# A merged front stage and attention scores computed two steps ahead, in a two-block transformer kernel on one core

## The chip, the cores and the metric

The kernel runs on one core of a Trainium2 chip: TensorE (PE), VectorE (DVE), ScalarE (ACT), GpSimd (POOL), the queue engine SyncE (SP) and 16 DMA engines. The metric is the time of one execution in microseconds, from the device; the median of three runs counts.

## The reference, cut to what matters

Two transformer blocks over 512 tokens of width 1024, in fp32. Only the first half of the first block is touched:

```python
mod = silu(c) @ w_ada + b_ada                     # 1024 x 6144
shift1, scale1, gate1, shift2, scale2, gate2 = split(mod, 6)
h = rms_norm(x, norm1_g) * (1 + scale1) + shift1
q_g, k_g, v_g, a_lr, r_g, q_s, k_s, v_s = split(h @ w_in)
log_a = log_sigmoid(a_lr @ w_gla_alpha + b) / 16
o_gla = rms_norm(gla_mixer(q_g, k_g, v_g, log_a)) * silu(r_g)   # gated linear attention, 4 heads
o_swa = rms_norm(swa_mixer(q_s, k_s, v_s, sinks))               # sliding window, 8 heads, 2 key heads
x = x + gate1 * (concat(o_gla, o_swa) @ w_out)
```

After that come the product-key expert layer (`peer_mixer`: a gather of expert rows), and the second block with its two attentions and its feed-forward. None of them is changed.

## The kernel before

Activations lie feature-first: `K.xres[:, k, :]` holds features 128k to 128k + 127 of all 512 tokens. Products with weights are made in three TensorE passes (`split_product`, L115 to L117): ScalarE rounds a weight tile to its high part (`high`, L269), GpSimd makes the low part (`lows`, L274), and high x high, high x low and low x high are added. `Columns` keeps three raw, three high and three low tiles; load n waits for low n - 3, high n for the product of tile n - 3.

The program is a row of stages, each a block in which every engine runs its own list, with a barrier between blocks. Those concerned:

1. `stage_setup` (0 to 51 us). SP loads x and the first 2048 columns of w_ada (shift1 and scale1) in eight tiles; ScalarE queues 23 small loads, among them c, which TensorE turns with all other vectors before ScalarE's Silu. TensorE turns x into `K.xres`. VectorE makes bias rows and masks, then adds up c times w_ada in 16 operations of 128x1024 (L480, L483), TensorE sums these over the partitions in 16 columns (L110), VectorE gets modT and g1.
2. `stage_in1` (51.6 to 229 us). The norm of x (`Norm`: squares on ScalarE L139, sums on TensorE L110, root L150 and L153, scale on VectorE L158), shift and rounding (L569), low part (L623). Then 16 column tiles (0 to 3 q and k of the linear attention, 4 the gate's rank, 5 to 12 r and the window's q, 13 and 14 its keys, 15 its values) and four row tiles for v_g. VectorE evicts tiles 4, 13, 14 and 15, ScalarE the others; tile n waits for the eviction of tile n - 2. Beside it VectorE adds up the other 4096 columns of w_ada in 32 operations (L632, L635) from a ring of two buffers, all of them ahead of its copy of the keys (L649) in its list; TensorE turns these sums after row tile c = 2.
3. `stage_mixers` (229 to 406 us). Two attentions are woven: `weave` sorts each engine's pieces by a place number that each generator yields. `Gla` has seven levels of 11 units: offsets of the log decay on VectorE (L753), two passes on ScalarE (L711, L713), factors qe and ke on VectorE (L789, L790), 16 products on TensorE (L110), taken under a mask into the scores (L762). After them an eighth product, decayed keys, states and outputs. `Swa` has 16 steps of 7.5 units, one block of 128 queries for two heads each: scores on TensorE; first() on VectorE: bias, row maximum, sink (L968 to L972); exps on ScalarE (L1007); second() on VectorE: sum, reciprocal and scaling of the probabilities (L976 to L979); turn on TensorE (L925), copy on ScalarE (L1015), product with the values on TensorE. The scores of step i + 1 are asked for at the start of step i and wait for the bias adds of step i; their two heads use partitions 0 to 63 and 64 to 127.

Then `stage_out1`, `stage_peer_scores` and the rest follow, unchanged.

## Time and profile before

| | us |
|---|---|
| median of 3 runs | 2811.97 |
| lowest, highest | 2810.17, 2816.26 |
| the profiled execution | 2816.42 |
| its span, first to last instruction | 2814.5 |
| `stage_setup` | 0 to 51.2 |
| `stage_in1` | 51.6 to 229.0 |
| `stage_mixers` | 229.0 to 406.2 |

All rows below are of the profiled execution. PE and the like with a q behind it are the engine's queue. A group's row gives line, engine, operation, out<-in, shapes, count, then busy time and mean ns of one, then how long the engine stood idle before these instructions and who ended that. A timeline row merges instructions alike: start, how long from the first's start to the last's end, count, and in brackets the idle time before it. Matmul records: an fp32 product is two records; on TensorE records overlap, so a mean can be longer than the distance from one to the next.

### The profile page before, as it was taken

To read this page: it belongs to the slowest core of one execution; us is meant where nothing else is said; L and a number is where in the kernel's file an instruction comes from. 1 tells how busy PE (TensorE), PEld (TensorE's weight loads), DVE (VectorE), ACT (ScalarE), POOL (GpSimd) and SP (SyncE) were. 2 spreads that over 40 slices of the span, in tenths; PEclk is the share of its full clock that TensorE was granted. 3 is DMA by queue.
4 is the path that set the end of the run, shared out by engine and by line. 5 is a ranking of instruction groups with operands and counts; after the bars stand their busy time and mean duration, and the time that the engine had idled before them with its cause. 6 is when DMAs were issued, how large, how long until landed. Compare 5 with 4: busy or idle time off the path is not lost. (4 is left out here: it accounts for less than half of the span.)

```text
span 2814.5 us, 22283 instructions
## 1 busy us (share of the span) xinstructions
PE 2132.3 (76%) x7265; PEld 1304.5 (46%) x7265; DVE 1515.5 (54%) x3605; ACT 674.4 (24%) x1202; POOL 1166.4 (41%) x774
## 2 busy tenths in 40 slices
PE   3875668861777777777788897767877997778899
PEld 2664446750322322222344443323336885646687
DVE  5535642119888678876788976555651112253111
ACT  2212343100000000000212112233214444444443
POOL 2320011311444444444466663322426885502687
PEclk7985578985999999999899998878998998879999
DMA  5640012334999999999999998977984664401465
GB/s 203 198 146 0 1 40 73 100 108 183 417 421 419 417 403 421 420 403 422 364 418 390 420 415 325 383 305 279 402 341 150 186 188 152 124 1 41 146 181 156
DMA packets 145864, 714.97 MB, mean 254 GB/s; under 512 B 13791, under 2 KB 39386, under 8 KB 79194
## 3 DMA queue, kind: packets, MB, share of 16 engines
q0 software_dynamic: 73728, 536.90, 46.8%
q1 hardware_dynamic: 69200, 172.38, 19.2%
q10 hardware_dynamic: 2826, 4.34, 0.4%
q8 instruction: 54, 0.88, 0.1%
q14 instruction: 56, 0.46, 0.1%
HBM read 701.77 MB, written 11.80 MB: 254 GB/s over the span
## 5 line engine op out<-in xcount | busy, mean ns | idle before, releaser
L1581 PE MATMUL ps<-uv_ring_a,expert_diag_a 128*128 128x512 f32 x2048 | 987.7, 633 | 392.9 <-DVE expert_diag_a L1472 392.8
L1364 POOL DMA_INDIRECT uv_ring_a<-in_peer_uv_dram,expert_idx x512 | 579.6, 1132 | 845.9 <-PE ps L1581 757.4
L1581 PEld LDWEIGHTS ps<-uv_ring_a,expert_diag_a 128*128 128x128 f32 x2048 | 396.3, 201 | 961.6 <-DVE expert_diag_a L1472 515.4
L1521 DVE CUSTOM_DVE_ANT_0 uv_ring_a<-uv_ring_a,x_rows 128x1024 f32<-128x1024 f32 x512 | 648.8, 1274 | 210.9 <-DMA uv_ring_a<-in_peer_uv_dram,expert_idx 208.8
L1652 POOL TENSOR_TENSOR w_low_b<-w_raw_b,w_high_b 128x1024 fp32r<-128x1024 f32 x98 | 234.7, 2397 | 236.3 <-ACT w_high_b L1646 234.9
L1564 ACT ACTIVATE expert_gelu_a<-expert_dot_a 128x2 f32<-128x2 f32 x256 | 52.1, 203 | 1054.4 <-DVE expert_dot_a L1521 1054.1
L1652 POOL TENSOR_TENSOR w_low_r<-w_raw_r,w_high_r 128x1024 fp32r<-128x1024 f32 x74 | 177.2, 2395 | 75.3 <-ACT w_high_r L1646 74.0
L1472 DVE TENSOR_SCALAR expert_diag_a<-ident,expert_weight_a 128x128 f32<-128x128 f32 x512 | 131.9, 314 | 15.0 <-PE ps L1581 5.6
L1646 ACT CAST w_high_b<-w_raw_b 128x1024 fp32r<-128x1024 f32 x98 | 102.8, 1051 | 119.0 <-PE ps L1665 119.0
L274 POOL TENSOR_TENSOR out_low<-out_raw,out_high 128x1024 fp32r<-128x1024 f32 x8 | 19.1, 2401 | 229.6 <-ACT out_high L269 229.6
L1646 ACT CAST w_high_r<-w_raw_r 128x1024 fp32r<-128x1024 f32 x74 | 77.9, 1055 | 85.2 <-PE ps L1665 85.0
L274 POOL TENSOR_TENSOR in_low<-in_raw,in_high 128x1024 fp32r<-128x1024 f32 x20 | 49.8, 2492 | 97.5 <-ACT in_high L269 97.5
L2387 DVE SCALAR_TENSOR_TENSOR ffn_silu_b<-ffn_silu_b,ps 128x256 f32<-128x256 f32 x22 | 9.2, 417 | 145.4 <-ACT ffn_silu_b L2369 145.4
L1663 PE MATMUL ps<-w_high_r,turned_high_r 128*128 128x512 f32 x208 | 82.2, 395 | 6.2 <-POOL w_low_r L1652 4.4
L1663 PE MATMUL ps<-w_high_b,turned_high_b 128*128 128x512 f32 x208 | 83.9, 403 | 3.8 <-DVE turned_low_b L1701 3.8
L2387 DVE SCALAR_TENSOR_TENSOR ffn_silu_r<-ffn_silu_r,ps 128x256 f32<-128x256 f32 x22 | 9.2, 418 | 140.7 <-ACT ffn_silu_r L2369 140.7
L220 POOL TENSOR_TENSOR peerq_low<-peerq_raw,peerq_high 128x1024 fp32r<-128x1024 f32 x16 | 38.0, 2378 | 110.8 <-ACT peerq_high L209 110.8
L1665 PE MATMUL ps<-w_high_b,turned_low_b 128*128 128x512 f32 x208 | 83.4, 401 | 0.0
L1664 PE MATMUL ps<-w_low_b,turned_high_b 128*128 128x512 f32 x208 | 83.4, 401 | 0.0
L1665 PE MATMUL ps<-w_high_r,turned_low_r 128*128 128x512 f32 x208 | 81.8, 393 | 0.0
L1664 PE MATMUL ps<-w_low_r,turned_high_r 128*128 128x512 f32 x208 | 81.7, 393 | 0.0
L115 PE MATMUL ps<-h_high,in_high 128*128 128x512 f32 (+1 forms) x128 | 52.1, 407 | 33.5 <-DVE kTd L649 17.2
(457 smaller groups left out, 3502.3 us busy)
## 6 DMA issues: line engine op xcount, KB each, us to landing
w_raw_r<-in_w_gu_dram SPq DMA_DIRECT2D x44, 512.0 KB, 3.8
w_raw_b<-in_w_gu_dram SPq DMA_DIRECT2D x44, 512.0 KB, 3.6
wada_rest<-in_w_ada_dram SPq DMA_DIRECT2D x32, 512.0 KB, 4.4
w_raw_a<-in_w_in_dram SPq DMA_DIRECT2D x24, 512.0 KB, 8.0
w_raw_b<-in_w_in_dram SPq DMA_DIRECT2D x24, 512.0 KB, 3.9
w_raw_r<-in_w_down_dram SPq DMA_DIRECT2D x22, 512.0 KB, 3.7
w_raw_b<-in_w_down_dram SPq DMA_DIRECT2D x22, 512.0 KB, 3.6
in_raw<-in_w_in_dram SPq DMA_DIRECT2D x20, 512.0 KB, 5.6
```

The source lines that it names most:

```text
L115: nc.tensor.matmul(out, w[0], x[0], start=first, stop=False)
L274: pool.tensor_tensor(self.lo[n % self.SPLIT][:, :], self.raw[n % self.RAW][:, :], self.hi[n % self.SPLIT][:, :].bitcast(F32), ALU.subtract ...
L1364: pool.indirect_dma_start(out=self.ring[:, n % self.RING, :], out_offset=None, in_=K.uv, in_offset=bass.IndirectOffsetOnAxis(ap=K.idx[self ...
L1472: dve.tensor_scalar(self.diag[q % self.DIAGS][:, :], K.ident[:, :], self.w[:, n % SLOTS:n % SLOTS + 1], None, ALU.mult).then_inc(self.s_di ...
L1521: dve.tensor_tensor_reduce(u, u, self.h[b][:, :], 1.0, 0.0, ALU.mult, ALU.add, self.a[:, s:s + 1]).then_inc(self.s_dot, 1)
L1564: act.activation(self.gl[:, c], self.a[:, c], ACT.Gelu).then_inc(self.s_gelu, 1)
L1581: ins = nc.tensor.matmul(self.bank(half), self.diag[q % self.DIAGS][:, :], self.ring[:, n % self.RING, D + 512 * half:D + 512 * half + 512 ...
L1646: act.copy(self.hi[n % self.SPLIT][:, :, :], self.raw[n % self.RAW][:, :, :]).then_inc(self.s_hi, 1)
L1652: pool.tensor_tensor(self.lo[n % self.SPLIT][:, :, :], self.raw[n % self.RAW][:, :, :], self.hi[n % self.SPLIT][:, :, :].bitcast(F32), ALU ...
L1663: nc.tensor.matmul(bank, rh, hi[:, kk, :], start=first and kk == 0, stop=False)
L1664: nc.tensor.matmul(bank, rh, lo[:, kk, :], start=False, stop=False)
L1665: ins = nc.tensor.matmul(bank, rl, hi[:, kk, :], start=False, stop=last and kk == self.KK - 1)
```

## The change

`stage_setup` and `stage_in1` become one block, `stage_front`:

- c is handed in as columns and loaded straight into its tile, as ScalarE's first load; the Silu follows on ScalarE before half of the small loads.
- w_ada's first part comes in 16 blocks of 128x1024, the scale half first, through a ring of six buffers lying in tiles that are written later; the other 32 blocks through a ring of three, then five.
- squares, sums and root of x follow the turning of x at once; GpSimd multiplies x by the inverse root (eight operations), and when g1 is there ScalarE scales and shifts in one operation and rounds in a second.
- the bias rows, masks and other constants are made between the sums; VectorE makes 28 of the 32 sums before the copy of the keys and four after the copy of the values; TensorE turns the sums after row tile c = 1.

In the mixers:

- the offsets and the zeroing of the level scores move from VectorE to GpSimd; TensorE's products of a level are four pieces half a unit apart.
- a step's two heads are now of the same half (0 to 63 or 64 to 127), their scores lie in one bank, the bank changes with the step, and the scores of step i + 2 are asked for in step i; one bias add serves both heads; the scaling of the probabilities moves from VectorE to ScalarE, before the turn.
- rows of w_out and of the window's norm gain are reordered on the host to fit.

```diff
+        ring1 = [rq_flat[:, D * r:D * r + D] for r in range(4)] + [qk_flat[:, D * r:D * r + D] for r in range(2)]
+        ring2 = own + [sums1[:, D * r:D * r + D] for r in range(2)]
+        MOD1 = [(k, c) for c in (1, 0) for k in range(KD)]
+        MOD2 = [(k, c) for k in range(KD) for c in range(4)]
...
+            for m, (k, c) in enumerate(MOD1):
+                if m >= len(ring1):
+                    sp.wait_ge(s_a1, m - len(ring1) + 1)
+                sp.dma_start(ring1[m % len(ring1)], I["w_ada"][0, k * P:(k + 1) * P, c * D:(c + 1) * D]) \
+                    .then_inc(s_w1[m % len(ring1)], 16)
+            for n in range(w.RAW):
+                w.load(sp, n)
...
+            turn = w.RAW
+            for m, (k, c) in enumerate(MOD2):
+                if m == len(own):
+                    sp.wait_ge(s_m1, 2)
+                if m >= len(ring2):
+                    sp.wait_ge(s_a2, m - len(ring2) + 1)
+                sp.dma_start(ring2[m % len(ring2)], I["w_ada"][0, k * P:(k + 1) * P, (2 + c) * D:(3 + c) * D]) \
+                    .then_inc(s_w2[m % len(ring2)], 16)
+                if m % 2:
+                    w.load(sp, turn)
+                    turn += 1
+            sp.dma_start(K.grow[:, :], I["b_ada"][0, 5 * D:6 * D].partition_broadcast(P)).then_inc(s_bg, 16)
+            for n in range(turn, len(w.src)):
+                w.load(sp, n)
...
+            pool.wait_ge(nm.s_inv, 1)
+            for k in range(KD):
+                pool.tensor_tensor(K.hT[:, k, :], K.xres[:, k, :], rs[:, :], ALU.mult).then_inc(s_xn, 1)
+            w.lows(pool, 0, 6)
+            pool.wait_ge(s_xn, KD)
+            step(pool.iota(dist, [[-1, 256]], base=P, channel_multiplier=1, allow_small_or_imprecise_dtypes=True))
...
+            w.lows(pool, 6, len(w.src))
...
+            act.dma_start(K.cact[:, :], I["c_columns"]).then_inc(s_c, 16)
...
+            act.wait_ge(s_c, 16)
+            act.activation(K.cact[:, :], K.cact[:, :], ACT.Silu).then_inc(s_silu, 1)
+            act.preload_act_table_set("natural_log_exp_and_others")
...
+            nm.squares(act, [(s_xe, k // 2 + 1) if k % 2 == 0 else (s_xd, k // 2 + 1) for k in range(KD)])
+            nm.root(act)
...
+                act.wait_ge(s_xn, k + 1)
+                act.activation(K.hT[:, k, :], K.hT[:, k, :], ACT.Identity, scale=K.g1[:, k:k + 1],
+                               bias=shift[k]).then_inc(s_h, 1)
+                act.wait_ge(s_h, k + 1)
+                act.copy(hi[:, k, :], K.hT[:, k, :]).then_inc(s_hh, 1)
...
+            for c in range(2):
+                pe.wait_ge(s_a1, KD * (c + 1))
+                for n in range(KD):
+                    o = KD * (1 - c) + n
+                    last = mm(nc, K.ps[7][:, o:o + 1], sums1[:, o * P:(o + 1) * P], K.ones[:, 0:1])
+                last.then_inc(s_m1, 1)
...
+                if c == 1:
+                    pe.wait_ge(s_a2, len(MOD2))
...
+            sums(0, len(MOD1), MOD1, ring1, s_w1, sums1, s_a1, 1)
+            dve.wait_ge(s_vt, 1)
+            dve.tensor_copy(K.vecT[:, :], K.ps[4][:, 0:P]).then_inc(s_ve, 1)
+            dve.wait_ge(s_ve, 1)
+            dve.wait_ge(s_m1, 2)
+            ch.link(dve.tensor_tensor(K.modT[:, 0:2 * KD], K.ps[7][:, 0:2 * KD], K.vecT[:, 0:2 * KD], ALU.add))
+            dve.scalar_tensor_tensor(out=K.g1[:, :], in0=K.modT[:, M_SCALE1:M_SCALE1 + KD], scalar=1.0,
+                                     in1=K.vecT[:, V_N1:V_N1 + KD], op0=ALU.add, op1=ALU.mult).then_inc(s_g1, 1)
             for k in range(KD):
                 dve.wait_ge(s_hh, k + 1)
-                dve.scalar_tensor_tensor(out=lo[:, k, :], in0=K.hT[:, k, :], scalar=shift[k],
-                                         in1=hi[:, k, :].bitcast(F32), op0=ALU.add, op1=ALU.subtract).then_inc(s_hl, 1)
-
-            def sums(first, last):
-                for m in range(first, last):
-                    k, c = MODS[m]
-                    dve.wait_ge(s_wm[m % 2], 16 * (m // 2 + 1))
-                    part, x = acc[:, c * D:(c + 1) * D], wada[m % 2][:, :]
-                    if k == 0:
-                        ins = dve.tensor_scalar(part, x, K.cact[:, 0:1], None, ALU.mult)
-                    else:
-                        dve.wait_ge(s_acc, m - 3)
-                        ins = dve.scalar_tensor_tensor(out=part, in0=x, scalar=K.cact[:, k:k + 1], in1=part,
-                                                       op0=ALU.mult, op1=ALU.add)
-                    ins.then_inc(s_acc, 1)
-            sums(0, 10)
+                dve.tensor_tensor(lo[:, k, :], K.hT[:, k, :], hi[:, k, :].bitcast(F32), ALU.subtract).then_inc(s_hl, 1)
...
+            rest(0, 8)
+            dve.wait_ge(s_pool, 13)
+            for h in range(SWA_H):
+                ch.then(dve.tensor_scalar(K.swab[:, h, :], dist, -(2.0 ** -(h + 1)), None, ALU.mult))
+            ch.sync()
...
+            rest(17, 28)
...
+            rest(28, len(MOD2))
...
+    def pool(self, pool):
+        NL, bT, ee = len(LEVELS), self.bT, self.ee
+        W2 = 2 * S
+        yield 0.0
+        pool.memset(self.sc[:, :, :], 0.0).then_inc(self.s_zero, 1)
+        yield 4.0
+        pool.wait_ge(self.s_b, 2)
+        for n in range(NL):
+            hs = LEVELS[n]
+            if n:
+                yield self.at(n - 1)
+            if n >= 2:
+                pool.wait_ge(self.s_qk, 2 * (n - 1))
+            b = self.spans(bT[:, :], hs)
+            pool.tensor_tensor(self.spans(ee[n % 2][:, :], hs), b,
+                               b[:, :, hs - 1:hs].to_broadcast([P, W2 // (2 * hs), 2 * hs]),
+                               ALU.subtract).then_inc(self.s_ref, 1)
+        yield self.at(NL) - 4.0
+        b = self.spans(bT[:, :], 64)
+        pool.wait_ge(self.s_qk, 2 * (NL - 1))
+        e = self.spans(ee[NL % 2][:, :], 64)
+        pool.tensor_tensor(e, b[:, :, P - 1:P].to_broadcast([P, W2 // P, P]), b, ALU.subtract).then_inc(self.s_ref, 1)
...
+            yield from level(n, qe[n % 2], ke[n % 2], self.at(n) + 5.0)
+        yield from level(NL, K.qkT[:, 0:2, :], K.qkT[:, 2:4, :], self.at(NL) + 2.0)
...
-            b, j = self.STEPS[i]
-            if i >= 1:
-                pe.wait_ge(self.s_b, 2 * i)
-            for e in range(2):
-                r = slice(64 * e, 64 * e + 64)
-                last = mm(nc, K.ps[4 + e][:, 0:256], K.rqT[r, 4 + j, b * P:(b + 1) * P],
-                          K.kTd[r, j // 2, b * P:b * P + 256])
+            b, t = self.STEPS[i]
+            g, e = divmod(t, 2)
+            r = slice(64 * e, 64 * e + 64)
+            if i >= 2:
+                pe.wait_ge(self.s_b, i - 1)
+            for h in range(2):
+                last = mm(nc, K.ps[4 + i % 2][:, 256 * h:256 * h + 256], K.rqT[r, 4 + 2 * g + h, b * P:(b + 1) * P],
+                          K.kTd[r, g, b * P:b * P + 256])
             last.then_inc(self.s_s, 1)
...
+        scores(1)
         for i in range(n):
-            if i + 1 < n:
-                yield self.at(i)
-                scores(i + 1)
+            if i + 2 < n:
+                yield self.at(i) + 1.0
+                scores(i + 2)
...
+            dve.tensor_tensor(sc[i % 2][:, :, :], K.ps[4 + i % 2][:, :].rearrange("p (h c) -> p h c", h=2), bias,
+                              ALU.add).then_inc(self.s_b, 1)
+            dve.wait_ge(self.s_b, i + 1)
...
-            ch.link(dve.reciprocal(sm[i % 2][:, :], sm[i % 2][:, :]))
-            for e in range(2):
-                last = dve.tensor_scalar(pr[i % 2][:, e, :], pr[i % 2][:, e, :], sm[i % 2][:, e:e + 1], None, ALU.mult)
-                if e == 0:
-                    ch.then(last)
-            last.then_inc(self.s_n, 1)
+            dve.reciprocal(sm[i % 2][:, :], sm[i % 2][:, :]).then_inc(self.s_r, 1)
...
+        def scale(i):
+            act.wait_ge(self.s_r, i + 1)
+            for h in range(2):
+                ins = act.activation(pr[i % 2][:, h, :], pr[i % 2][:, h, :], ACT.Copy, scale=sm[i % 2][:, h:h + 1])
+            ins.then_inc(self.s_n, 1)
...
+            yield self.at(i) + 3.5
+            scale(i)
```

## Rows read from the trace of the kernel before

**Rows 1.** The page's first line: span and instructions.
```profile
span 2814.5 us, 22283 instructions
```

**Rows 2.** Busy time in stretches: from:to, length, engines, then granted clock, DMA share, GB/s.
```profile
0.00:78.90 78.90, 21.77 (x83) 16.17 (x83) 46.44 (x72) 21.58 (x31) 16.07 (x25) 0.69 0.47 181
78.90:165.60 86.70, 86.63 (x364) 67.67 (x364) 44.43 (x30) 21.12 (x26) 32.21 (x13) 0.97 0.71 230
229.00:406.20 177.20, 108.65 (x616) 80.70 (x616) 104.66 (x224) 62.65 (x144) 0.00 (x0) 0.62 0.00 1
370.00:380.00 10.00, 8.22 (x50) 5.79 (x50) 1.64 (x5) 4.61 (x8) 0.00 (x0) 1.00 0.00 0
```

**Rows 3.** Timeline of stage_setup: x turned, w_ada sums, columns.
```profile
9.13 5.40 PE L431 MATMUL ps<-ident,hT 128*128 128x128 f32 x32 [9.13 <-DMA hT<-in_x_dram]
...
22.29 12.03 DVE L483 SCALAR_TENSOR_TENSOR mixT<-wada,cact,mixT 128x1024 f32<-128x1024 f32 x10
...
43.74 6.99 PE L110 MATMUL ps<-ones,mixT 128*128 128x1 f32 x32 [24.00 <-DVE mixT L483]
```

**Rows 4.** Timeline from the norm of x to the first projection.
```profile
54.00 8.61 PE L110 MATMUL ps<-hT,ones 128*128 128x512 f32 x16 [3.28 <-ACT hT L139]
...
64.03 9.57 DVE L158 SCALAR_TENSOR_TENSOR hT<-xres,g,rs 128x512 f32<-128x512 f32 x8 [12.89 <-ACT rs L153]
...
70.98 3.37 ACT L569 ACTIVATE h_high<-hT,modT 128x512 fp32r<-128x512 f32 x5 [2.02 <-DVE hT L158]
...
78.95 0.80 PE L115 MATMUL ps<-h_high,in_high 128*128 128x512 f32 x1 [16.34 <-DVE h_low L623]
```

**Rows 5.** VectorE beside GpSimd: timeline at 88 us; line 158's durations, min/median/max in ns.
```profile
88.82 2.39 POOL L274 TENSOR_TENSOR in_low<-in_raw,in_high 128x1024 fp32r<-128x1024 f32 x1 [18.42 <-ACT in_high L269]
...
89.29 3.00 DVE L635 SCALAR_TENSOR_TENSOR mixT<-wada_rest,cact,mixT 128x1024 f32<-128x1024 f32 x1 [1.81 <-DMA wada_rest<-in_w_ada_dram]
...
L158 DVE SCALAR_TENSOR_TENSOR hT<-xres,g,rs x8: 739/742/2839, 64.0 to 72.9; 128x512 f32<-128x512 f32 x8
```

**Rows 6.** Groups of TensorE from 78.9 to 229: the projections' first pass.
```profile
L115 PE MATMUL ps<-h_high,in_high 128*128 128x512 f32 (+1 forms) x128 | 52.1, 407 | 33.5 <-DVE kTd L649 17.2 <-DVE h_low L623 16.3
```

**Rows 7.** Groups of the mixers, 229 to 412 us.
```profile
L762 DVE COPY_PREDICATED gla_scores<-lmask,ps 128x512 f32<-128x512 int32 x32 | 20.4, 721 | 0.0
...
L925 PE MATMUL ps<-ident,swa_p 128*128 128x128 f32 x64 | 16.8, 412 | 43.4 <-DVE swa_p L979 43.4
L1007 ACT ACTIVATE swa_p<-swa_s,swa_negmax 128x256 f32<-128x256 f32 x32 | 16.0, 499 | 66.9 <-DVE swa_sink L972 66.9
L968 DVE TENSOR_TENSOR swa_s<-ps,swab 128x256 f32<-128x256 f32 x32 | 12.1, 420 | 55.4 <-PE ps L110 55.4
...
L970 DVE TENSOR_REDUCE swa_negmax<-swa_s 128x2 f32<-128x512 f32 x16 | 11.0, 686 | 0.5
...
L979 DVE TENSOR_SCALAR swa_p<-swa_p,swa_sum 128x256 f32<-128x256 f32 x32 | 9.9, 351 | 0.6
L1015 ACT COPY swa_pT<-ps 128x512 f32<-128x512 f32 x16 | 9.3, 582 | 25.4 <-PE ps L925 25.4
...
L789 DVE TENSOR_TENSOR gla_qe<-qkT,gla_e 128x1024 f32<-128x1024 f32 x7 | 8.5, 1221 | 0.0
L753 DVE TENSOR_TENSOR gla_e<-bT 128x1024 f32<-128x1024 f32 x7 | 8.5, 1219 | 0.0
L713 ACT ACTIVATE gla_e<-gla_tmp 128x1024 f32<-128x1024 f32 x7 | 7.4, 1057 | 0.2
```

**Rows 8.** TensorE's timeline in the mixers: first level, one level with its step, eighth product.
```profile
245.82 4.49 PE L110 MATMUL ps<-gla_qe,gla_ke 64*128 64x128 f32 x29 [1.15 <-DVE gla_ke L790]
...
325.60 4.24 PE L110 MATMUL ps<-gla_qe,gla_ke 64*128 64x128 f32 x32 [2.58 <-DVE gla_ke L790]
329.77 1.11 PE L925 MATMUL ps<-ident,swa_p 128*128 128x128 f32 x4
330.81 1.13 PE L110 MATMUL ps<-swa_pT,vs 128*64 128x128 f32 x8
331.87 1.23 PE L110 MATMUL ps<-kTd,rqT 64*128 64x256 f32 x4
...
351.65 4.49 PE L110 MATMUL ps<-qkT 64*128 64x128 f32 x29
```

More of the change, by code:

```diff
@@ L269, in high, with lows @@
         act.copy(self.hi[n % self.SPLIT][:, :], self.raw[n % self.RAW][:, :]).then_inc(self.s_hi, 1)
-    def lows(self, pool):
-        for n in range(len(self.src)):
+    def lows(self, pool, first=0, last=None):
+        for n in range(first, len(self.src) if last is None else last):
             pool.wait_ge(self.s_hi, n + 1)
@@ new lines, in rest @@
+            def rest(first, last):
+                sums(first, last, MOD2, ring2, s_w2, sums2, s_a2, 4)
+            dve.wait_ge(s_silu, 1)
+            sums(0, len(MOD1), MOD1, ring1, s_w1, sums1, s_a1, 1)
[4 more added lines that the diff above has]
+            ch.link(dve.tensor_tensor(K.modT[:, 0:2 * KD], K.ps[7][:, 0:2 * KD], K.vecT[:, 0:2 * KD], ALU.add))
```

387 lines of the change are left out of this document (155 added, 232 removed).

## The prediction, made blind

> **What bounds the kernel now.** I read the page first for the span [rows 1], then the busy time by stage [rows 2]: the reader is to see that everything the change touches lies before 406 us, that TensorE is idle for most of the first 79 us, then busy throughout up to 165.6, and is granted little more than the low clock (0.5 is 1.2 GHz, 1.0 is 2.4 GHz) in the mixers. What comes after 406 us waits for the mixers' end, each stage behind a barrier, so a microsecond saved before it is a microsecond of the span, as long as nothing later changes. The profiled execution took 2816.42 us around its span of 2814.5, and the median of three runs is 2811.97; I sum in the span and take the same difference off the median.
>
> Three things hold the front. (1) The first projection starts at 78.95 [rows 4]. Before it one chain runs with a block boundary in the middle: the w_ada sums on VectorE, back to back; 16 columns on TensorE, 7.0 us [rows 3]; then, only now, the norm of x: its sums on TensorE, a scale pass of 9.6 us on VectorE, rounding on ScalarE, low parts [rows 4]. (2) A pause of 17.2 us behind 165.6: tile 15 waits for the key copy kTd, which stands behind all 32 sums of the rest of w_ada in VectorE's order [rows 6]. (3) In the mixers TensorE and VectorE take turns: VectorE idles 55.4 us for scores, TensorE 43.4 us for scaled probabilities, ScalarE 66.9 us for the row maximum [rows 7].
>
> **The front, part by part.** The norm of x needs no modulation, and the change runs it while w_ada arrives. Squares start when x is turned. x lands at 9.13 as before [rows 3]. ScalarE now waits for c and does the Silu and two table loads before 13 more small loads, so I put its first copy at 13, the squares at 16.4 to 20.8, the sums at 17 to 25 (8.6 us [rows 4]), the inverse root at 26. VectorE's last copy of x is then at 17 and its sums start there: 14 at 1.2 us (12.03 for ten [rows 3]) and two at 0.75, 18.3 us, ending at 35.5 if nothing disturbs them. The loads don't pace them: x, 2 MB, landed within 8.3 us of its issue, a block of 0.5 MB then takes at most 2.1 us, six are there before the first sum, and the other ten end by 18 + 3.5 + 9 x 2.1 = 40 at worst.
>
> They are disturbed. From 26 on GpSimd multiplies x by the inverse root, eight operations of 128x512; one of 128x1024 took 2.39 us [rows 5], so 1.2 each, an estimate. A sum that starts inside such an operation took 3.00 us where one alone takes 1.2: it began 0.47 us after GpSimd's, waited until that was over, and then did its own work [rows 5]. Of VectorE's eight scale operations, 0.74 each, the longest took 2.84 with GpSimd's lows beside them [rows 5]; GpSimd's two lows there let one operation of VectorE pass between them, so I let the engines alternate. About eight sums are left at 26, so both streams end near 26 + 8 x (1.2 + 1.2) = 45. The Trainium skill, "SBUF — State Buffer", section "Who interferes with whom", says a VectorE instruction with two SBUF inputs and a GpSimd one that reads SBUF exclude each other for the whole instruction. It speaks against this change, which moves two-input work to GpSimd; the trace agrees with it. Were it not so, the 45 would be 36.
>
> After 45: eight columns in place of sixteen, 3.5 us (half of [rows 3]); modT and g1, 0.5; then for each of eight tiles ScalarE shifts and scales (0.7 us, [rows 4]) and, after a wait on that, rounds (0.6): 1.25 us each, 10 us; one low part, 1. The first projection starts at 45 + 3.5 + 0.5 + 10 + 1 = **60**; 51 without the exclusion, 66 if c lands late by 6.
>
> From there the old stretch was 229.0 - 78.95 = 150.1 us, of which 17.2 idle and about 2 the restart at the low clock: 130.9. The work is the same, so the mixers start near 191, **38 us** earlier (47 to 30). This holds only if the pause goes. A tile takes 86.7 / 15 = 5.8 us [rows 2], tile 13 ends at first projection + 81. VectorE has by then 28 sums: at 1.64 us each (held now and then by GpSimd) 46, another 8 for bias rows, masks, copies, and waits for alrT and the gates until + 43, after which 17 sums and 5 us of masks are 33: + 77. The slack is 4 us. The last four sums come behind the value copy and end near + 99; TensorE asks for them after the second row tile, near + 103. New queueing: GpSimd's lows from tile 6 stand behind iota and two selects of swab, which wait for VectorE's bias rows; the selects of 128x2048 are taken at 2 each, so low 6 is ready near + 33 and asked for at + 36. On SP the loads of w_in 3 stand behind GpSimd's first low and those after it behind w_ada's ring; needed 10 us later at the earliest. The moved constants lie under the sums, at no cost; if that cover were gone they would cost their 5 us.
>
> **The mixers.** From the first level product (245.8) to the eighth (351.65) there are seven periods of 15.1 us [rows 8], with 1.47 attention steps each (7.5 against 11 in the order by place). I walk one period by program order with row durations: levels on TensorE 4.2 to 4.4, turn and values 2.1, scores 1.2 [rows 8]; VectorE: first() 1.8 (two bias adds of 0.42, the reduce, two small), takes 4 x 0.64, q and k factors 2.35; ScalarE: exps 1.25, the level's two passes 2.1, copy 0.6 [rows 7]. The same walk of the old order gives 14.1 for a short period (one step beside it), under the mean of 15.1 as it should be.
>
> Removed from VectorE: the offsets (eight of 1.22), the memset, the scaling (two of 0.35 a step) [rows 7]. Added to ScalarE: two Copy passes over 256 columns a step. No row shows that form alone; the exps of that size are 0.50 with their accumulation and overlap, so 0.75 for two, between 0.6 and 1.2. Added to GpSimd: the offsets, 2.39 by [rows 5], asked for a level ahead, so off the chain but for the first; each holds one small two-input operation of VectorE by about 1 us. Both scores of a step now use the same 64 rows of the array. Before, the pairs used both halves and ran side by side, four records of 256 columns in 1.23 us. The turn's four records of 128 columns, one after the other, took 1.11 [rows 8], some 0.21 to 0.25 apart; at twice the columns four are about 1.9 us, 0.7 more (0 to 0.9).
>
> A short period then: level 4.4, scores 2.0, turn 1.1, values 1.1, scores 2.0 on TensorE, 10.6, while qe and ke are ready at 9.3. A long one: factors 9.3, first() to 12.1, level to 15.0, turn 16.1, copy 16.7, the level's passes 18.8, exps 20.0, scaling 20.8, turn 21.9, values 23.0 and the next level: 12.4. The mean is 11.5; TensorE is not always at the low clock, I take 11.3: 7 x 3.8 = 27 us. Start: the memset and the first offset leave VectorE's chain, one offset on GpSimd (2.4) enters it, - 2. End: steps without a level beside them took scores 1.2, first() 1.8, the rest of the step on VectorE 0.9, turn and values 2.1, 6.0; now exps, scaling, turn and copy, 1.25 + 0.75 + 1.1 + 0.6 and waits, 4.3; two such steps, - 3 (the norms after them stay). **32 us** (20 to 42).
>
> Sum: 2814.5 - 38 - 32 = 2744.5; median 2811.97 - 70 = **2742**.
>
> **Rivals.** *B, the clock rises.* TensorE would be busy some 85% of the mixers instead of 61% [rows 2]. From 370 to 380, where it was busy for 8.2 of 10 us, 1.0 was granted; over the mixers it was 0.62. At 2.4 GHz the level is 2.3, the step's work about half, and the long chain of ScalarE is left: 9.6 a period, 12 more, and 3 to 5 in the rest: 2725. The Trainium skill, "TensorE: Matmul & The Clock Gate", section "HAM oscillation — how this bites in real kernels", says the clock falls when waits break up TensorE's work; by that rule closing the waits gives the high level back. *C, the new orders hold less.* The slack of 4 us is used up and TensorE waits 7 for kTd, the Copy passes take 1.2 and stand between exps and the next turn, so a period is 13: 7 + 12 less: 2762. *E, it doesn't do what it says:* the full wait for kTd and half of the alternation stay, 17 + 27 less: 2786. *D, slower.* The offsets on GpSimd run over spans of 2 to 128 elements with the middle one repeated; the row of 2.39 is for plain rows. Over 11 us such an operation would set the period; from 11.3 + 70 / 7 = 21.3 us the seven periods eat the whole gain, and at 28 the kernel takes 2742 + 7 x 16.7 = 2859. Against it: VectorE's offsets, of the same shapes, took no longer than its plain products, 1.22, and the nearest row of GpSimd is a ninth of the threshold.
>
> **Chances.** Forecast 0.57 (2732 to 2752 by its own bounds), B 0.18, C 0.18, E 0.04, D 0.03. 2720 to 2768 takes in the first three with their ends. A measurement can tell about 0.2% (6 us) from no change: faster 0.96, same 0.01, slower 0.03.
>
> **What would show it.** First projection (h_high, in_high) at 60, mixers' first product at 191, no idle time of TensorE behind kTd; sums of 2.4 us between 26 and 45; level products 11.3 apart; score records one after the other; offsets on GpSimd near 2.4. A first projection at 51 would mean no exclusion; a granted clock near 1.0 in the mixers is B; ScalarE busy where TensorE waits for swa_p is C. I would be wrong if stages after the mixers changed their length.

## The result, and the profile after

| | before | the change |
|---|---|---|
| median of 4 runs, us | 2814.11 | 2742.39 |
| lowest, highest | 2810.17, 2820.75 | 2736.24, 2749.12 |
| ratio, 95% interval | | 0.9743 [0.9712, 0.9774] |
| span of the profiled execution | 2814.5 | 2747.3 |
| first projection | 78.95 | 61.46 |
| mixers' first product | 229.29 | 194.87 |
| first level product | 245.82 | 209.47 |
| eighth product | 351.65 | 275.45 |
| next stage's first product | 415.51 | 347.85 |
| from there to the end | 2399.0 | 2399.4 |

The forecast was 2742 us. The profiled execution is the slowest of its four, 2749.12 us. The front gives 34.4 us (forecast 38), the mixers, taken from their first product to the next stage's first, 186.2 - 153.0 = 33.2 us (forecast 32), and nothing behind them moves. The line that answers [rows 1], from the page, and those that answer [rows 2], with the same columns; the three stretches are front, projections up to 15 tiles, mixers:

```profile
span 2747.3 us, 22283 instructions
```

```profile
0.00:61.40 61.40, 20.05 (x81) 15.53 (x81) 37.59 (x36) 24.51 (x36) 28.74 (x29) 0.72 0.72 259
61.40:148.20 86.80, 86.74 (x370) 68.22 (x371) 59.39 (x60) 22.52 (x29) 43.16 (x18) 0.98 0.73 259
194.80:338.60 143.80, 106.97 (x616) 80.52 (x616) 90.36 (x167) 75.64 (x176) 17.15 (x9) 0.70 0.00 1
```

The projections take the same time; in the mixers TensorE is busy for 74% (61% before) at a mean granted clock of 0.70 (0.62). Next the timeline of the change's front, which answers [rows 3 to 5]:

```profile
10.12 0.58 ACT L467 COPY xres<-ps 128x512 f32<-128x512 f32 x1 [2.53 <-PE ps L505]
15.05 4.27 ACT L139 ACTIVATE mixT<-xres 128x512 f32<-128x512 f32 x8
23.69 0.63 ACT L153 ACTIVATE rs<-rs 128x512 f32<-128x512 f32 x1
24.40 16.32 POOL L429 TENSOR_TENSOR hT<-xres,rs 128x512 f32<-128x512 f32 x8 [19.22 <-ACT rs L153]
40.69 8.91 POOL L274 TENSOR_TENSOR in_low<-in_raw,in_high 128x1024 fp32r<-128x1024 f32 x3
...
30.89 4.30 DVE L574 SCALAR_TENSOR_TENSOR vg<-qkT,cact,vg 128x1024 f32<-128x1024 f32 x2
35.29 9.79 DVE L574 SCALAR_TENSOR_TENSOR vg<-rqT,cact,vg 128x1024 f32<-128x1024 f32 x4
45.14 3.58 PE L110 MATMUL ps<-ones,vg 128*128 128x1 f32 x16 [14.91 <-DVE vg L574]
49.03 0.58 DVE L587 SCALAR_TENSOR_TENSOR g<-modT,vecT 128x8 f32<-128x8 f32 x1
49.65 0.81 ACT L475 ACTIVATE hT<-hT,modT,g 128x512 f32<-128x512 f32 x1 [8.43 <-DVE g L587]
50.50 0.62 ACT L478 CAST h_high<-hT 128x512 fp32r<-128x512 f32 x1
51.02 0.81 ACT L475 ACTIVATE hT<-hT,modT,g 128x512 f32<-128x512 f32 x1
61.46 0.80 PE L115 MATMUL ps<-h_high,in_high 128*128 128x512 f32 x1 [12.75 <-DVE h_low L591]
```

The reader sees sums of 2.1 us instead of 1.3 from 24.4 on (the last, behind GpSimd's first low part, takes 3.2), GpSimd's eight products one each 2.04 us (16.32 / 8) in between, and ScalarE's pair repeating every 1.37 us (51.02 - 49.65). Two groups answer [rows 6]: no wait for kTd is left, and before the columns of the modulation (`K.vs`, the window's values, is the tile waited for) TensorE waits 1.15 us.

```profile
L115 PE MATMUL ps<-h_high,in_high 128*128 128x512 f32 (+1 forms) x128 | 51.0, 398 | 12.7 <-DVE h_low L591 12.7
```

```profile
165.42 12.07 PE L110 MATMUL ps<-ones,mixT 128*128 128x1 f32 x64 [1.15 <-DVE vs L633]
```

The mixers' groups of the change, which answer [rows 7]:

```profile
L110 PE MATMUL ps<-kTd,rqT 64*128 64x256 f32 x64 | 22.7, 495 | 2.8 <-PEq L331 2.8
L736 DVE COPY_PREDICATED gla_scores<-lmask,ps 128x512 f32<-128x512 int32 x32 | 22.2, 730 | 6.4 <-PE ps L110 6.3
L992 ACT ACTIVATE swa_p<-swa_s,swa_negmax 128x256 f32<-128x256 f32 x32 | 15.9, 498 | 22.1 <-DVE swa_sink L963 22.1
L999 ACT ACTIVATE swa_p<-swa_p,swa_sum 128x256 f32<-128x256 f32 x32 | 14.3, 494 | 1.4 <-DVE swa_sum L968 1.4
L913 PE MATMUL ps<-ident,swa_p 128*128 128x128 f32 x64 | 14.2, 360 | 26.7 <-ACT swa_p L999 26.7
L804 POOL TENSOR_TENSOR gla_e<-bT 128x1024 f32<-128x1024 f32 x7 | 13.5, 1928 | 38.0 <-DVE gla_ke L758 32.2 <-DVE bT L746 5.8
L958 DVE TENSOR_TENSOR swa_s<-ps,swab 128x512 f32<-128x512 f32 x16 | 11.0, 686 | 20.6 <-PE ps L110 20.5
L962 DVE TENSOR_TENSOR swa_negmax<-swa_negmax,negsink 128x2 f32<-128x2 f32 x16 | 5.8, 364 | 0.6
```

The three waits that made the alternation shrink: VectorE's for scores from 55.4 to 20.5 us, TensorE's for probabilities from 43.4 to 26.7, ScalarE's for the row maximum from 66.9 to 22.1.

### The profile page after: what moved, and what is told of

The parts are those of the page before. It is cut to its first block and busy times, and to the rows that moved or that the text cites. A ratio compares the mean times of both kernels' runs of the same rounds, so it can differ in the third digit from the quotient of the medians.

```text
span 2747.3 us, 22283 instructions
## 1 busy us (share of the span) xinstructions
PE 2135.1 (78%) x7265; PEld 1306.6 (48%) x7265; DVE 1504.9 (55%) x3540; ACT 689.8 (25%) x1240; POOL 1195.3 (44%) x791
## 5 line engine op out<-in xcount | busy, mean ns | idle before, releaser
L1361 POOL DMA_INDIRECT uv_ring_a<-in_peer_uv_dram,expert_idx x512 | 568.9, 1111 | 852.9 <-PE ps L1578 764.1
L274 POOL TENSOR_TENSOR in_low<-in_raw,in_high 128x1024 fp32r<-128x1024 f32 x20 | 56.2, 2814 | 58.9 <-ACT in_high L269 58.8
```

The costliest lines, as they stand in the source:

```text
L274: pool.tensor_tensor(self.lo[n % self.SPLIT][:, :], self.raw[n % self.RAW][:, :], self.hi[n % self.SPLIT][:, :].bitcast(F32), ALU.subtract ...
L1361: pool.indirect_dma_start(out=self.ring[:, n % self.RING, :], out_offset=None, in_=K.uv, in_offset=bass.IndirectOffsetOnAxis(ap=K.idx[self ...
```

## The experiments

All times are medians, with lowest and highest behind them; the kernel before stood between 2817.22 and 2819.16 us in these comparisons. "Levels" is the stretch from the first level's product to the eighth product, "tail" from there to the next stage's first product, "mixers" from their first product to the next stage's. Granted clocks are means over the levels and over 40 us that begin 9 us behind the eighth product. The expectations count the mixers' length to their own last instruction instead, some 9.2 us less (144 there is 153 here).

| kernel | first projection | mixers start | levels, clock | tail, clock | mixers |
|---|---|---|---|---|---|
| before | 78.95 | 229.29 | 105.8, 0.55 | 63.9, 0.83 | 186.2 |
| the change | 61.46 | 194.87 | 66.0, 0.80 | 72.4, 0.50 | 153.0 |
| after_again | 61.69 | 195.23 | 66.1, 0.80 | 61.9, 0.84 | 142.6 |
| change_again | 61.16 | 194.44 | 65.8, 0.80 | 72.4, 0.50 | 152.8 |
| front_only | 60.53 | 195.02 | 105.2, 0.58 | 63.6, 0.87 | 185.3 |
| mixers_only | 79.2 | 232.10 | 70.3, 0.69 | 74.5, 0.50 | 159.4 |
| x_on_vector | 55.02 | 189.18 | 70.6, 0.66 | 72.4, 0.50 | 157.3 |
| offsets_on_vector | 61.23 | 194.45 | 70.0, 0.70 | 63.4, 0.83 | 147.5 |
| scaling_on_vector | 61.44 | 194.91 | 66.8, 0.76 | 54.9, 0.90 | 136.3 |
| sums_first | 61.58 | 197.45 | 74.4, 0.59 | 63.3, 0.83 | 152.0 |
| tail_reordered | 62.48 | 196.18 | 69.9, 0.66 | 56.8, 0.83 | 141.1 |
| scores_one_step | 61.86 | 195.32 | 106.5, 0.53 | 71.0, 0.71 | 192.1 |
| x_scaling_vector | 54.92 | 189.25 | 71.0, 0.57 | 54.0, 0.87 | 139.2 |
| order_alone | 61.73 | 195.24 | 69.4, 0.62 | 54.8, 0.87 | 139.0 |

### The two halves, and the change again

```diff
--- the change
+++ front_only: the three parts of the mixers as before
-class Gla, class Swa, stage_mixers (of the change)
+class Gla, class Swa, stage_mixers (of the kernel before)
--- the change
+++ mixers_only: the front as before
-stage_front
+stage_setup, stage_in1
```

> The new front stage with the old mixers. If the two halves of the change add up: first projection at 61.5, mixers start at 194.5, mixers 177 us long as before, so 35 us less than before (2779). Rival: the mixers in the changed kernel gain part of their time from the new front (what the engines did before they start), then their length differs from 177 by more than 3 us.

> The old two front stages with the new mixers. If the halves add up: the mixers start at 229.0 as before and take 144 us (134 if the clock of their last third is up), so 33 us less (2781), or 43 at most. Rival as for front_only.

> The changed kernel once more, unaltered, for a second trace. In the first one the granted clock was 0.50 from 284 to 324 us although TensorE was busy throughout; before, the same work at 360 to 380 had 0.83 and 1.0. Theory 'chance': the clock of that stretch differs from execution to execution; a second trace shows it near 1.0 there in at least some executions, and the mixers then take about 134 us instead of 144. Rival 'order': the new order itself leaves that stretch at the low clock; the second trace shows 0.50 there again and mixers of 144. Either way the front ends within 1 us of 194.5 and the ratio is 0.974.

Measured against 2818.24: front_only 2780.03 (2778.46 to 2784.06), ratio 0.9866 [0.9843, 0.9889]; mixers_only 2780.97 (2776.09 to 2792.59), 0.9863 [0.984, 0.9885]; the change 2737.92 (2735.91 to 2748.69), 0.9728 [0.970, 0.9757]. The parts add: 38.2 + 37.3 = 75.5 us against 80.3 together and 71.7 in the first comparison. The front alone leaves the mixers' length alone (185.3 against 186.2), so that rival is out for this half. The median of mixers_only is the one expected, but its trace isn't: it is of the slowest execution, 2792.59, where the mixers start at 232.10, not 229, and take 159.4 us, 6 more than expected, with the tail at 0.50. In after_again the tail ran at 0.84 and the mixers took 142.6, which is 133.4 in the expectation's count and theory 'chance' (134).

### The exclusion of VectorE and GpSimd in the front

```diff
--- the change
+++ x_on_vector
             pool.memset(K.vs[:, 0, :], 0.0).then_inc(s_pad, 1)
-            pool.wait_ge(nm.s_inv, 1)
-            for k in range(KD):
-                pool.tensor_tensor(K.hT[:, k, :], K.xres[:, k, :], rs[:, :], ALU.mult).then_inc(s_xn, 1)
-            w.lows(pool, 0, 6)
             pool.wait_ge(s_xn, KD)
+            w.lows(pool, 0, 6)
...
             sums(0, len(MOD1), MOD1, ring1, s_w1, sums1, s_a1, 1)
+            dve.wait_ge(nm.s_inv, 1)
+            for k in range(KD):
+                dve.tensor_tensor(K.hT[:, k, :], K.xres[:, k, :], rs[:, :], ALU.mult).then_inc(s_xn, 1)
```

> The changed kernel with the eight products of x and the inverse root moved from GpSimd to VectorE, after its 16 sums; GpSimd's first lows wait for them. Theory 'exclusion': the eight sums that took 2.3 us each beside GpSimd take 1.2, the sums end at 36 in place of 45, the eight products (0.7 each) lie under TensorE's columns, modT comes at 42 in place of 48.8 and the first projection at 54.5 in place of 61.5: 7 us less than the changed kernel. Rival 'loads': the sums were slow because their blocks came late; then they still end near 45, the products come on top, and the first projection is at 65 or later.

2739.56 us (2732.8 to 2745.47), 0.9715 [0.9685, 0.9744]. Its timeline:

```profile
30.47 5.45 DVE L571 SCALAR_TENSOR_TENSOR vg<-rqT,cact,vg 128x1024 f32<-128x1024 f32 x4
35.84 4.89 DVE L581 TENSOR_TENSOR hT<-xres,rs 128x512 f32<-128x512 f32 x8
41.18 2.00 DVE L587 SCALAR_TENSOR_TENSOR g<-modT,vecT 128x8 f32<-128x8 f32 x1
...
40.82 7.40 POOL L274 TENSOR_TENSOR in_low<-in_raw,in_high 128x1024 fp32r<-128x1024 f32 x3 [35.63 <-DVE hT L581]
...
55.02 0.79 PE L115 MATMUL ps<-h_high,in_high 128*128 128x512 f32 x1 [15.47 <-DVE h_low L591]
```

The last four sums take 5.45 us where they took 9.79 beside GpSimd, and the sums end at 35.8, against 45.0: the forecast's two values for a front without and with the exclusion were 36 and 45. The eight products cost VectorE 4.9 us, and the first projection still starts 6.4 us earlier. g1, eight columns wide, took 2.00 us here and 0.58 in the change: it started 0.36 us behind GpSimd's first low part. The total shows nothing of it, 2739.56 beside the change's 2737.92 in the same comparison, where 7 us less was expected: in the trace the mixers take 157.3 us against 142.6 in after_again, with levels and tail granted 0.66 and 0.50 against 0.80 and 0.84, and that gives it back.

### The order of the sums

```diff
--- the change
+++ sums_first
-            rest(17, 28)
+            rest(17, len(MOD2))
...
-            rest(28, len(MOD2))
```

> The change with all 32 sums of w_ada ahead of the key columns' copies, as the kernel before orders them; the ring of buffers and everything else stays. The forecast's account: the last four sums end at the first half + 99, some 3 us behind the product that frees the key columns' bank, so that TensorE pauses 3 to 5 us there (17.2 us before the change) and the mixers start as much later: 198-200 us instead of 195, the time 2742-2746. The rival, that it was the earlier and deeper ring that took the pause away and the order adds nothing: no pause at the keys, mixers start at 195 (within 1 us), time the change's.

2748.39 us (2743.27 to 2749.03), 0.9743 [0.9724, 0.9763]. TensorE, at the keys:

```profile
149.53 0.50 PE L115 MATMUL ps<-h_high,in_high 128*128 128x512 f32 x1 [2.02 <-DVE kTd L625]
```

The pause comes back, but with 2.0 of its 17.2 us; the mixers start 2.6 us later, 197.45, a little under the 3 to 5 expected. The median is above the 2742 to 2746 expected, with levels of 74.4 us at 0.59. So moving four sums behind the value copy is worth 2 us of the pause, and 15 went with the rest of the front: the earlier and deeper ring, the other places of the constants. No run takes these apart, but the traces point to the ring: among these sums VectorE waited 42.3 us for blocks of w_ada in the kernel before and 3.8 in sums_first, and the last of the 32 ends 87 us behind the first projection instead of 103.

### What shortened the levels

```diff
--- the change
+++ scores_one_step
         scores(0)
-        scores(1)
         for i in range(n):
-            if i + 2 < n:
-                yield self.at(i) + 1.0
-                scores(i + 2)
+            if i + 1 < n:
+                yield self.at(i)
+                scores(i + 1)
--- the change
+++ offsets_on_vector
         for n in range(NL):
+            if n + 1 < NL:
+                yield self.at(n)
+                offsets(n + 1)
...
-            pool.tensor_tensor(self.spans(ee[n % 2][:, :], hs), b,
--- the change
+++ scaling_on_vector
-            dve.reciprocal(sm[i % 2][:, :], sm[i % 2][:, :]).then_inc(self.s_r, 1)
+            ch.link(dve.reciprocal(sm[i % 2][:, :], sm[i % 2][:, :]))
+            for e in range(2):
+                last = dve.tensor_scalar(pr[i % 2][:, e, :], pr[i % 2][:, e, :], sm[i % 2][:, e:e + 1], None, ALU.mult)
...
-            yield self.at(i) + 3.5
-            scale(i)
--- scaling_on_vector
+++ order_alone: with offsets_on_vector's edit too
```

> The change with its offsets back on VectorE, at the places they had before; GpSimd only zeroes the scores' tile. Theory 1 (VectorE sets the level's period, as the sum of the forecast has it): VectorE is busy 55.1 of the 66.1 us between the first level's product and the eighth's and would get 7 operations of 1.22 us there, less some 3 us that its small operations are now held by GpSimd: that stretch goes from 66 to 72-75 us, the time from 2738-2742 to 2745-2750. Theory 2 (the period is a chain of products, copies and scores through all engines, and VectorE's 11 us of idle time take the offsets in): stretch 65-68 us, time within 2 us of the change's.

> The change with the probabilities' scaling back on VectorE, two operations of 0.35 us a step right behind the reciprocal, as before; ScalarE's pair of 0.9 us a step goes. Theory 1 (VectorE's total counts): nine steps lie in the levels, VectorE gets 9 x 0.75 = 7 us more there and the stretch from the first level's product to the eighth's goes from 66 to 71-73 us; the steps behind the levels, where ScalarE and VectorE both have time, stay. The time is 2744-2749. Theory 2 (each step's chain counts): the chain gets 0.15 us shorter a step and loses a hop between two engines, so the stretch is 64-67 us and the time the change's or up to 3 us less.

> The change with each step's scores asked for one step ahead again, at the place the kernel before has; the two score banks, the one add of 512 columns and ScalarE's scaling stay. Theory 1 (asking two steps ahead is what took VectorE's wait for scores out of the levels): the scores again come one product later than VectorE could add them, VectorE's wait for them in the mixers goes from 10-20 us to 25-40 us, the stretch from the first level's product to the eighth's goes from 66 (at a granted clock of 0.80) or 70-74 (at 0.59 to 0.66) to 76-84 us, and the time to 2750-2758. Theory 2 (one add for two heads and a second bank for the scores already free the bank early enough, and the step ahead adds nothing): the stretch lies on the same line of length against granted clock as the change's and its siblings', and the time within 3 us of the change's.

> The change's front, and of the change to the mixers only the order: scores two steps ahead with a bank each and one add for two heads. Offsets and scaling are both back on VectorE; GpSimd only zeroes the scores' tile. With scores one step ahead and the rest of the change kept, the levels took 106.5 us, no less than before the change. Theory 1 (the order alone is worth nearly all, and taking work off VectorE nothing at a granted clock that leaves TensorE as busy): the levels take 70 to 76 us, the mixers' first product to the next stage's 138 to 146 us, the median is 2733-2742, at or below the change's 2738-2746. Theory 2 (once the order is right VectorE's total sets the period, which then needs both moves): VectorE gets some 62 + 8 us of work in the levels, is busy over 90% of them, they take 78 us or more, and the median is 2745-2752.

Measured: offsets_on_vector 2742.91 (2738.12 to 2745.74), 0.9729 [0.9708, 0.975]; scaling_on_vector 2732.04 (2730.09 to 2734.53), 0.9692 [0.9674, 0.971]; scores_one_step 2786.16 (2782.37 to 2788.57), 0.9885 [0.9868, 0.9901]; order_alone 2737.33 (2731.89 to 2739.41), 0.971 [0.9693, 0.9726]. The levels of the last two, one line each, then their groups of VectorE's bias add from 190 to 345 us (the columns of [rows 2] and [rows 7]):

```profile
209.93:316.43 106.50, 73.07 (x386) 58.91 (x385) 51.91 (x102) 40.99 (x98) 11.02 (x6) 0.53 0.00 1
...
L957 DVE TENSOR_TENSOR swa_s<-ps,swab 128x512 f32<-128x512 f32 x14 | 9.7, 689 | 52.6 <-PE ps L110 52.0 <-DVE gla_state L778 0.4
```

```profile
210.05:279.47 69.42, 63.41 (x384) 51.97 (x384) 63.22 (x127) 32.21 (x77) 0.00 (x0) 0.62 0.00 1
...
L960 DVE TENSOR_TENSOR swa_s<-ps,swab 128x512 f32<-128x512 f32 x16 | 11.0, 687 | 8.5 <-PE ps L110 8.5
```

With the scores one step ahead the levels take 106.5 us, as long as before the change, though VectorE has only 51.9 us of work in them: within the levels it waits 51.6 us for scores (42.2 before the change, 0.1 in the change). With the scores two steps ahead and the offsets and the scaling back on VectorE, 63.2 us of work, they take 69.4, with 0.2 us of that wait. I had expected 76 to 84 us and a time of 2750 to 2758 for the first, so even theory 1 was much too mild.

Some parts of the new order are in both kernels and were not taken apart: two heads of the same half, a bank for each step, one add for two heads, a level's products in four pieces. Without the two steps they are worth nothing in the levels (106.5 against 105.8); whether the two steps would do as much without them isn't shown. The timeline of scores_one_step shows why so much hangs on it:

```profile
226.29 4.11 PE L110 MATMUL ps<-gla_qe,gla_ke 64*128 64x128 f32 x24 [4.17 <-DVE gla_ke L758]
230.34 1.11 PE L913 MATMUL ps<-ident,swa_p 128*128 128x128 f32 x4
231.38 1.13 PE L110 MATMUL ps<-swa_pT,vs 128*64 128x128 f32 x8
232.44 2.07 PE L110 MATMUL ps<-gla_qe,gla_ke 64*128 64x128 f32 x8
234.31 1.91 PE L110 MATMUL ps<-kTd,rqT 64*128 64x256 f32 x4
...
236.26 0.69 DVE L957 TENSOR_TENSOR swa_s<-ps,swab 128x512 f32<-128x512 f32 x1 [9.75 <-PE ps L110]
```

The next scores stand behind the level's products, and those wait for VectorE's factors. So VectorE makes the factors, then waits 9.75 us for TensorE's level, step and scores to go by, and only then adds the bias; TensorE waits for it in its turn. A step further ahead the scores lie ready when the factors are done.

The other two edits gave little in the levels. With the offsets on VectorE they take 70.0 at 0.70, between the ranges of the two theories (72 to 75, 65 to 68) and in line with the change's own mixers at like clocks (70.3 at 0.69, 70.6 at 0.66); the time is the change's, which is nearer to theory 2. With the scaling on VectorE they take 66.8 at 0.76, hardly longer either, though VectorE's work in them rises from 55.1 to 62.4 us; that is theory 2 too, and the median is 6 us below the lowest of the change's three medians, more than the 3 expected. In order_alone all three of theory 1's numbers are met or bettered. VectorE is busy for 91% of its levels, as theory 2 had it, but the 78 us or more that this was to cost did not come. No trace has these levels at 0.80, so what VectorE's work would cost at the higher clock is open.

In the tail the scaling on ScalarE costs something. TensorE's timeline in scaling_on_vector, then in after_again, two waits of each:

```profile
284.32 0.66 PE L913 MATMUL ps<-ident,swa_p 128*128 128x128 f32 x4 [1.45 <-DVE swa_p L970]
...
304.29 0.66 PE L913 MATMUL ps<-ident,swa_p 128*128 128x128 f32 x4 [1.64 <-DVE swa_p L970]
```

```profile
284.41 1.12 PE L913 MATMUL ps<-ident,swa_p 128*128 128x128 f32 x4 [3.50 <-ACT swa_p L999]
...
305.02 1.11 PE L913 MATMUL ps<-ident,swa_p 128*128 128x128 f32 x4 [2.35 <-ACT swa_p L999]
```

On ScalarE the scaling of a step stands behind the next step's exponentials and the copies of gla_kdn. The tail is 61.9 us at 0.84 with it and 54.9, 54.0 and 54.8 at 0.87 to 0.90 in the three kernels without it. The waits for swa_p behind the eighth product add up to 7.8 and 3.3 us (3.50 + 2.35 + 1.49 + 0.42 and 1.45 + 1.64 + 0.17), so 4.5 of the 7 us are theirs; the rest goes with the clock.

### The tail's clock

```diff
--- the change
+++ tail_reordered (step 11 alone)
-        yield self.at(NL) + 7.0
+        yield self.at(NL) + 5.45
...
+            if i == 11:
+                yield self.at(i) + 0.4
+                second(i)
...
+            if i == 11:
+                yield self.at(i) + 1.9
+                scale(i)
```

The three places are those of ScalarE's copies of gla_kdn, of VectorE's sum and reciprocal, and of ScalarE's scaling.

> At step 11 of the windowed attention alone, VectorE's sum and reciprocal and ScalarE's scaling go ahead of the next step's bias and exponentials, and ScalarE's two copies of gla_kdn too. The change's traces show TensorE waiting 3.5 to 5 us there (280 to 285 us), and the granted clock at 0.50 for the 40 us behind it in three of four traces, 0.83 in the fourth. Theory 1 (the clock's fall is started by that pause): the pause is under 1.5 us, the granted clock over the 40 us behind is 0.8 or more in the trace, the stretch from the eighth product to the mixers' end takes 48-52 us instead of 63, and the median is 2724-2730 with little spread. Theory 2 (the level in that stretch varies from one execution to the next, whatever is ahead of it): only the pause itself is won, 2 to 3 us, the median is 2735-2740 and runs spread as before over 2732-2748.

> The change itself on the same chip as the two others, for differences of a few us. If the stretches at the low level of TensorE's clock in the mixers come by chance, one of its times lies 5 us or more from another, and the trace shows either 62 or 72 us from the eighth product to the next stage's first (both have been seen, at 0.84 and at 0.50); the instruction times on the other engines are the same to 1% in either. If it is a property of the kernel, the trace shows 0.50 there and times within 3 us of each other.

tail_reordered 2740.12 us (2737.96 to 2740.46), 0.9717 [0.97, 0.9735]; the change on another occasion, change_again, 2746.24 (2740.56 to 2749.26), 0.974 [0.9722, 0.9759]. The 9 us behind the eighth product and the next 40, in the change, after_again and tail_reordered:

```profile
275.45:284.45 9.00, 5.27 (x49) 4.61 (x48) 5.41 (x11) 3.04 (x10) 0.00 (x0) 0.94 0.00 0
284.45:324.45 40.00, 36.59 (x156) 26.09 (x155) 7.75 (x26) 14.73 (x38) 0.00 (x0) 0.50 0.00 1
```

```profile
275.93:284.93 9.00, 5.27 (x49) 4.61 (x48) 5.41 (x11) 3.05 (x10) 0.00 (x0) 0.94 0.00 0
284.93:324.93 40.00, 32.21 (x171) 21.19 (x169) 12.52 (x33) 23.18 (x52) 0.00 (x0) 0.84 0.01 1
```

```profile
280.55:289.55 9.00, 8.60 (x88) 7.21 (x87) 7.57 (x18) 3.63 (x11) 0.00 (x0) 1.00 0.01 2
289.55:329.55 40.00, 27.62 (x132) 17.25 (x130) 13.68 (x32) 24.20 (x53) 0.00 (x0) 0.83 0.01 4
```

The first two are the same program and alike up to 285 us (levels of 66.0 and 66.1 us, both at 0.80, the next 9 us equal in every engine to 0.01), and then one stays at the low level for 40 us in which TensorE is busy for 36.6, and the other doesn't: 10.5 us of difference in the tail. So the level there isn't set by the program alone, and the spread of its times, 2735.91 to 2749.26 over twelve, is of this size. In tail_reordered the pause is gone (busy 8.60 of 9 us) and the clock is 0.83, as theory 1 wants, and its four times lie within 2.5 us; but 0.83 was also granted in sums_first and offsets_on_vector, which kept the pause with 3.50 us, and the median is 2740, as theory 2 has it. The tail's 56.8 us are in neither theory's range. That the pause starts the fall isn't shown; what is shown is a tail of 56.8 us against 61.9 at the same clock. Its front came 1 us late (first projection 62.48) and its levels took 3.9 us more at 0.66, which is where that gain went in the total.

### The two best edits together

```diff
--- scaling_on_vector
+++ x_scaling_vector: with x_on_vector's edit too
```

> The two parts together that shortened their own stretch when done alone: x times the inverse root on VectorE (first projection 6.5 us earlier) and the probabilities' scaling on VectorE (the steps behind the levels shorter by 4.5 us of TensorE's waits and some more at the same clock). If both keep: first projection at 55, mixers start 189, mixers' first product to the next stage's 136 to 145 us by the clock that is granted there, span 2724 to 2733, median 2724-2728. The rival, that the clock falls longer where the start of the mixers comes earlier, as in the trace with x on VectorE alone: the levels take 71-74 us at 0.6 and the median is 2730-2735, no better than the scaling alone.

2733.12 us (2724.28 to 2733.47), 0.97 [0.9684, 0.9716], 13 us under the change on the same chip and with no time in common. The median is in the rival's range, and the levels ran at 0.57 (71.0 us) as the rival says; yet the first projection, the mixers' start and their length are the first theory's, and the profiled execution, the fastest of its four with a span of 2722.3, is a little under its range. With scaling_on_vector (2732.04) it is the fastest kernel here.

## Why the prediction was right

**The start of the front** was put 1.7 to 3 us late: ScalarE's first copy came at 10.12, not 13, the inverse root at 24.3, not 26. **The exclusion**, the choice on which 9 us hung, held: engines alternating, sums ending at 45.0 as forecast. Two errors cancel in that: the product of 128x512 costs some 0.85 us between two sums (2.04 less 1.2), not 1.2, but GpSimd's three low parts, which I had not counted there, stand right behind the products and hold the last sums. The rule of the Trainium skill, "SBUF — State Buffer", section "Who interferes with whom", that VectorE with two SBUF inputs and a reading GpSimd exclude each other, spoke against this part of the change; x_on_vector bears it out (sums ending at 35.8 without GpSimd's products, 45.0 with them). **The chain of h**: the shift with scale, two operands from memory, is 0.81 us, not 0.7, so 1.37 a tile and 11, not 10; g1 took 0.58. Hence 61.46 for 60.

**From there to the mixers** 133.4 us for 130.9. The key pause is gone as forecast, but the slack of 4 us was right by two errors that cancel. The 28th sum ended at 141.9, 80.5 us behind the first projection and not 77: the 17 sums after the gates took 1.87 us each, not 1.64. And the prediction wanted the key copy when tile 13 ends, + 81, while tile 15, which waits for it, starts one tile later, at 147.5. With the copy's 0.7 us that leaves 4.9; the four sums took 6.9 in sums_first, which gives its pause of 2.0. The last four sums ended near + 99 as forecast. Missed are 1.15 us of waiting for `K.vs`, whose copy stands behind them and behind two operations on the bias rows (2.77 and 0.91 us), and the 32 columns, 12.07 us where they took 10.4 before: TensorE was granted 0.58 there, 0.67 before.

**The levels** are where the mechanism was right and the size wrong: 66.0 us, 39.8 less and not 27. The walk by program order gave a period of 11.3 at little more than the low clock. Measured were 10.6 (74.4 / 7) at 0.59 and 9.4 (66.0 / 7) at 0.80. Between the traces at 0.59 and at 0.80, of mixers with the same code, lie 8.4 us, so of the 13 us that were missed some 8 are the clock, which is rival B's price, and 5 the walk. It added TensorE's and VectorE's pieces of a period as if each waited for the last in full; the scores asked for two steps ahead let them overlap further, which fits VectorE's wait for scores, 0.1 us in the levels, but is argued, not measured by itself. What the prediction did not say, and what the runs show, is that the order does nearly all of this: it named the offsets and the scaling first, as work removed from VectorE, and they are worth nothing measurable in the levels. The start gave 1.9 us (16.5 to 14.6), with 2 forecast.

**GpSimd's offsets** took 1.93 us, under the 2.39 of the plain row, a tenth of rival D's 21.3. They do hold VectorE's small operations: L962 has a mean of 364 ns, and 161 where the offsets are on VectorE. **The Copy passes** are 0.9 us for two, inside the bounds of 0.6 and 1.2. **The scores** are 1.9 us for four at the low level, as worked out from the turn (1.91 in the timeline above), and 1.0 at the high one.

**The tail** is the term with the wrong sign in the profiled execution: 72.4 us against 63.9, + 8.5 where - 3 was forecast. At a like clock it is 61.9, - 2. So the total came out right by two things that nearly cancel there: levels 13 us shorter than forecast and a tail 11.5 us longer, 10.5 of which another execution of the same program doesn't have. That the sum landed on 2742 within a microsecond is luck in this part; the range was needed.

**Rival B** named the rule of the Trainium skill, "TensorE: Matmul & The Clock Gate", section "HAM oscillation — how this bites in real kernels", that waits which break up the work bring the clock down, and closing them brings it back. In the levels the change's trace agrees (0.55 to 0.80), but x_scaling_vector was granted 0.57 there with TensorE busy for 67.2 of 71.0 us, and sums_first 0.59 with 66.9 of 74.4; for the 40 us at 0.50 with TensorE busy for 36.6 the rule does not account either. So that the closed waits raised the clock isn't shown.

Rivals C, E and D did not come about: no wait at the keys, 34.9 of VectorE's 55.4 us of waiting for scores gone, offsets at 1.93. One thing that C feared does hold, but behind the levels: the Copy passes stand between the exponentials and the next turn, for 4.5 us of waits in the tail. C's own sum gives 2761, not 2762, on which nothing hangs.

## What to carry to other kernels

Where two engines take turns in one program order, look first for the product that could be issued a step earlier, ahead of one that waits for the other engine; that one place in the order is worth 40 us here (2786.16 against 2746.24), and 21 us of work taken off the busier engine (32 scalings of 0.35, eight offsets of 1.22) gave nothing that could be measured in the total (order_alone, 2737.33). Work given to an idle engine can lengthen the chain elsewhere: the scaling on ScalarE costs the tail 4 us or more, and the product on GpSimd costs VectorE more than doing it itself. And where TensorE's clock moves between its two levels, compare stretches by length and granted clock together, with a second trace of the same kernel, before a few microseconds are put down to an edit.

## What the hardware showed that was not expected

- The same program was granted 0.50 in one execution and 0.84 in another over the same 40 us, with the levels before it alike; in the first TensorE was busy for 36.6 of the 40 us without the clock rising. Of the seven traces with the change's orders in the tail (the change three times, mixers_only, x_on_vector, sums_first, and offsets_on_vector but for its last offset) four show the low level there. In the levels 0.57 was granted with TensorE busy for 95% of the time (x_scaling_vector) and 0.80 with 78% (the change). Why is open.
- GpSimd's subtraction of a repeated middle element over 128x1024 took 1.93 us where plain rows took 2.39, much the same for spans of 2 to 128 (L804, 1.89 to 2.01 us over seven).
- An operation of eight columns on VectorE took 2.00 us when it started behind one of GpSimd's of 2.4 us, and 0.58 otherwise; one of two columns (L962) took 364 ns on the mean beside GpSimd's offsets and 161 without them. How small the held operation is did not help it.
